# A hybrid decoder layer on one core: the same mixing stage with fewer and narrower products, another order, and a TensorE that starts on zeros

## What is computed

```python
z = rmsnorm(x, mix_norm) @ w_in                      # (256, 1024) @ (1024, IN_WIDTH)
log_f = log_sigmoid(ff + fox_f_bias)                 # 8 columns of z; c = cumsum(log_f)
logit[t,s] = q_t.k_s/8 + c[t] - c[s]                 # q, k: rms-normalised per head
S_t = S_{t-1} diag(w_t) + (S_{t-1} a_t) b_t^T + v_t k_t^T ;  y_t = S_t r_t   # S_0 = 0
y = (y - mean(y)) * rsqrt(var(y) + GN_EPS)           # per head, over its 64 value columns
y = (y * ln_w + ln_b + bonus) * g                    # bonus is from v as it is
x = x + concat([fox_out * sigmoid(fog), y]) @ w_out
logits = rmsnorm(x, moe_norm) @ w_router + b_router  # top 4 of 32 experts per token
x = x + sum of gate * expert(x)                      # clamped SwiGLU, 1024 -> 2 x 1024 -> 1024
x = x + sigmoid(rmsnorm(x) @ w_ple_gate) * (p @ w_ple_proj);  return rmsnorm(x)
```

## Time and profile before

| | |
|---|---|
| median of 3 runs | 1184.32 us (1183.87 to 1185.1) |
| the profiled execution, its own time | 1185.83 us |
| its span | 1184.0 us |
| PE busy | 1136.0 us (96%), 7064 matmuls |
| DVE busy | 283.3 us (24%) |
| ACT busy | 173.2 us (15%) |
| read from HBM | 433.06 MB, 367 GB/s over the span |

### The profile page before, as it was taken

How to read it: one execution, slowest core, us unless ns; L and a number is a source line. 1 busy time by engine, 2 the same in 40 slices (tenths; PEclk the granted TensorE clock), 3 DMA queues, 4 the chain that set the end, 5 groups by cost and what they waited for, 6 DMA issues and landing times.

```text
span 1184.0 us, 16869 instructions
## 1 busy us (share of the span) xinstructions
PE 1136.0 (96%) x7064; PEld 480.0 (41%) x7064; DVE 283.3 (24%) x578; ACT 173.2 (15%) x319; POOL 0.2 (0%) x4
## 2 busy tenths in 40 slices
PE   7999999999999999999999999999999999998997
PEld 6888856433333333333333333333333333332334
DVE  2454734421111111111211211111111111111123
ACT  3322523210100100000010000000000000000015
POOL 0000000000000000000000000000000000000000
PEclk9999999999999999999999999999999999999999
DMA  9751036599999999999999999999999999999970
GB/s 376 324 214 74 22 126 232 218 354 412 427 427 428 427 428 428 429 428 425 430 429 427 429 427 425 429 426 429 428 428 428 429 428 428 429 428 428 427 320 35
DMA packets 34027, 434.76 MB, mean 367 GB/s; under 512 B 4032, under 2 KB 4288, under 8 KB 6976
## 3 DMA queue, kind: packets, MB, share of 16 engines
q1 hardware_dynamic: 33984, 434.13, 87.3%
HBM read 433.06 MB, written 1.05 MB: 367 GB/s over the span
## 4 chain that ended last, share of the span: by engine, by line
PE 48%; DMA 35%; DVE 1%; issue 0%; ACT 0%; SPq 0%; DVEq 0%
DMA ring<-in_we 35%; PE PS L929 33%; PE PS L877 3%; PE PS L892 2%; PE PS L1033 2%; PE PS L753 2%; PE PS L946 1%; PE PS L884 1%; PE PS L980 1%; PE PS L815 0%; PE PS L955 0%; PE PS L548 0%; PE PS L820 0%; PE PS L900 0%; PE PS L776 0%
## 5 line engine op out<-in xcount | busy, mean ns | idle before, releaser
L929 PE MATMUL PS<-ring,FV 128*64 128x512 f32 x2276 | 508.1, 595 | 21.3 <-DMA ring<-in_we 21.3
L929 PEld LDWEIGHTS PS<-ring,FV 128*64 128x64 f32 x2276 | 156.7, 137 | 353.5 <-issue 303.5
L929 PE MATMUL PS<-B,FV 128*64 128x512 f32 x772 | 175.0, 595 | 6.2 <-DMA B<-in_we 6.2
L929 PEld LDWEIGHTS PS<-B,FV 128*64 128x64 f32 x772 | 53.4, 137 | 112.7 <-issue 99.8
L536 PE MATMUL PS<-hT,ring 128*128 128x256 f32 x416 | 93.0, 382 | 0.9 <-ACT hT L1086 0.6
L536 PEld LDWEIGHTS PS<-hT,ring 128*128 128x128 f32 x416 | 78.1, 190 | 12.2 <-ACT hT L1086 0.8
L1573 DVE TENSOR_SCALAR rz<-con,lora 128x64 f32<-128x64 f32 x30 | 7.6, 255 | 305.4 <-PE PS L929 305.4
L1340 DVE TENSOR_TENSOR FV<-PS,prm 128x512 f32<-128x512 f32 x32 | 22.1, 692 | 184.6 <-PE PS L884 184.6
L1655 DVE TENSOR_SCALAR hT<-PS 128x512 f32<-128x512 f32 x32 | 22.1, 692 | 176.8 <-PE PS L929 176.8
L877 PE MATMUL PS<-xq,rz 128*64 128x512 f32 x256 | 62.0, 605 | 0.0
L892 PE MATMUL PS<-B,rz 64*128 64x512 f32 x248 | 61.6, 615 | 0.0
(11 more groups left out here) (273 smaller groups left out, 683.6 us busy)
## 6 DMA issues: line engine op xcount, KB each, us to landing
ring<-in_we SPq DMA_DIRECT2D x135, 2048.0 KB, 23.4
B<-in_we SPq DMA_DIRECT2D x48, 2048.0 KB, 27.6
ring<-in_wz SPq DMA_DIRECT2D x7, 2048.0 KB, 22.7
ring<-in_we SPq DMA_DIRECT2D x14, 1024.0 KB, 7.9
ring<-in_wo SPq DMA_DIRECT2D x2, 2048.0 KB, 7.8
ring<-in_wgate SPq DMA_DIRECT2D x2, 2048.0 KB, 38.8
stash<-in_we SPq DMA_DIRECT2D x1, 2048.0 KB, 13.4
xq<-in_x SPq DMA_DIRECT2D x2, 512.0 KB, 5.3
```

Source lines behind the costliest of these rows:

```text
L929: mm = pe.matmul(PS[64 * h:64 * h + 64, bank_, :], lhs(4 * (q % 2) + k), early[u] if u < units else w[:, k, h, :], start=(first and k == 0 ...
```

## The change

- SP issues both halves of x ahead of `prm`; the first weight piece is issued when the first half of x has landed, the second when the second half has.
- TensorE does 12 products of 128x128 on the zeroed state right after VectorE has zeroed it, and nobody reads them. The wait for all of `hT` goes; the products of `z(0)` wait one by one.
- "bp" leaves its place after z 18 and becomes the second product of "q" 4. Its copy by ScalarE follows "q" 4's.
- The forget-gate columns: weights of eight products side by side (32 columns wide) write four strips of 32 partitions; ScalarE copies the strips, and one product with a 0/1 matrix `fold8` sums the wanted rows ("ff"). z 26 moves ahead of z 22, which is split.
- "t" and "tt": each update only computes the 32 of 64 columns that the level changes, and VectorE adds 512 instead of 1024 columns (strided). "q" k now waits for the second update (`tt`) of the level before, where it waited for the first.
- ScalarE uses one table set (`natural_log_exp_and_others`) for all logarithms and exponentials of the levels, and loads `exp_and_others` once, before the tanh of "fg".
- Chunk 0 leaves out the products with the zero state in "x" and "y".
- The means of y go: "q" 2's second product, which turned v by the identity, turns it by (identity - 1/64) (`centre`, made by VectorE), so that each head's v and with it y comes out centred; the sums, the wait for them and the subtraction are left out.
- Before the routing's last fold there is a product on the first weights of expert 1, which nobody reads; the wait for these weights stands just ahead of it.

The diff, without the tables of step names and without context:

```diff
...
@@ -83,2 +83,2 @@
-MIX_ORDER = [("z", 18), ("bp", 0), ("z", 19), ("ma", 0), ("z", 20), ("aa", 0), ("z", 21), ("z", 22),
-             ("q", 1), ("z", 26), ("qsq", 0), ("ffa", 0), ("ffe", 0), ("t", 1), ("fc", 0), ("qss", 0),
+MIX_ORDER = [("z", 18), ("z", 19), ("ma", 0), ("z", 20), ("aa", 0), ("z", 21), ("z", 26), ("zh", 22),
+             ("q", 1), ("ff", 0), ("qsq", 0), ("z", 22), ("ffa", 0), ("ffe", 0), ("t", 1), ("qss", 0), ("fc", 0),
...
@@ -194,0 +195,6 @@
+        def q_at(k):
+            return 13 if k < 5 else 4
+
+        def level_half(i, k, bit):
+            return b16(i).rearrange("p g (a s b) -> p g a s b", s=2, b=1 << k)[:, :, :, bit, :]
+
@@ -220,0 +227 @@
+        centre = XU[:, 0, 0:CH]
@@ -232,0 +240 @@
+        ff4 = fv2[:, 768:1024]
@@ -235 +243 @@
-            return 2 if n == NZ + 2 else n % 4
+            return 3 if n == NZ else 2 if n == NZ + 2 else n % 4
@@ -334 +341,0 @@
-            sp.dma_start(prm[:, :], t["prm"]).then_inc(s_prm, 16)
@@ -335,0 +343 @@
+            sp.dma_start(prm[:, :], t["prm"]).then_inc(s_prm, 16)
@@ -340,0 +349,2 @@
+                if n < TB:
+                    sp.wait_ge(s_x[n], 16)
@@ -500,0 +511,3 @@
+            pe.wait_ge(s_dve, dve_at["init"])
+            for _ in range(12):
+                pe.matmul(PS[:, 7, 0:P], S[:, 0, 0:P], S[:, 1, 0:P], start=True, stop=True)
@@ -509,2 +521,0 @@
-            pe.wait_ge(s_act, act_at[f"hT{KD - 1}"])
-            pe.wait_ge(s_dve, dve_at[f"hT{KD - 2}"])
@@ -515 +526 @@
-                    pe.wait_ge(s_act, act_at[f"z{n - 4}"])
+                    pe.wait_ge(s_act, act_at[f"z{NZ - 7 if n == NZ else n - 4}"])
@@ -534,0 +546,4 @@
+                    if n == 0 and k % 2:
+                        pe.wait_ge(s_act, act_at[f"hT{k}"])
+                    elif n == 0:
+                        pe.wait_ge(s_dve, dve_at[f"hT{k}"])
@@ -538 +553,3 @@
-                        mm = pe.matmul(PS[0:NHEAD, z_bank(n), 0:SEQ], wff[:, k, :], hT[:, k, :], **flags)
+                        rows = slice(NE * (k % 4), NE * (k % 4) + NE)
+                        four = wff[:, k // 4 * 4:k // 4 * 4 + 4, :].rearrange("p k n -> p (k n)")
+                        mm = pe.matmul(PS[rows, z_bank(n), 0:SEQ], four, hT[:, k, :], start=(k < 4), stop=(k >= 4))
@@ -587,0 +605,3 @@
+            def centred(rows, g):
+                return centre[rows, :]
+
@@ -596,0 +617,3 @@
+            def columns(i, k, bit):
+                return lambda rows, g: level_half(i, k, bit)[rows, g]
+
@@ -606,4 +629 @@
-                if kind == "bp":
-                    pe.wait_ge(s_dve, dve_at["tildes"])
-                    fin(per_head((6, blocks(4), eye, 0)), "bp0")
-                elif kind == "ma":
+                if kind == "ma":
@@ -611 +631 @@
-                    pe.wait_ge(s_act, act_at["bp"])
+                    pe.wait_ge(s_dve, dve_at["tildes"])
@@ -615,0 +636,3 @@
+                elif kind == "ff":
+                    pe.wait_ge(s_act, act_at[f"z{NZ}"])
+                    fin(pe.matmul(PS[0:NHEAD, z_bank(NZ), SEQ:2 * SEQ], c_("fold8"), ff4, start=True, stop=True), "ff0")
@@ -630 +653 @@
-                        pe.wait_ge(s_dve, dve_at[f"t{k - 1}"])
+                        pe.wait_ge(s_dve, dve_at[f"tt{k - 1}"])
@@ -635,2 +658,4 @@
-                        pe.wait_ge(s_act, act_at[f"z{NZ}"])
-                        beside = ((2, blocks(2), eye, 0),)
+                        pe.wait_ge(s_act, act_at["ffh"])
+                        pe.wait_ge(s_act, act_at["z22"])
+                        pe.wait_ge(s_dve, dve_at["cen"])
+                        beside = ((2, blocks(2), centred, 0),)
@@ -639,0 +665,4 @@
+                    elif k == 4:
+                        pe.wait_ge(s_act, act_at["kp"])
+                        pe.wait_ge(s_dve, dve_at["tt3"])
+                        beside = ((4, blocks(4), eye, 0),)
@@ -646,5 +675 @@
-                    if k > 1:
-                        pe.wait_ge(s_dve, dve_at[f"tt{k - 1}"])
-                    else:
-                        pe.wait_ge(s_act, act_at["kp"])
-                    fin(per_head((6, blocks(14), blocks(4), 1), (4, blocks(4), blocks(14), 0)), f"t{k}")
+                    fin(per_head((6, blocks(14), columns(q_at(k), k, 0), 1), (7, blocks(q_at(k)), columns(14, k, 1), 0), n=CH // 2), f"t{k}")
@@ -653,2 +678 @@
-                    pe.wait_ge(s_dve, dve_at[f"tt{k - 1}"])
-                    fin(per_head((4, blocks(4), blocks(14), 0)), f"tt{k}")
+                    fin(per_head((7, blocks(q_at(k)), columns(14, k, 1), 0), n=CH // 2), f"tt{k}")
@@ -720,0 +745 @@
+                        pe.wait_ge(s_act, act_at["bp"])
@@ -723 +748 @@
-                    mm = both(STATE_X, [(ar_(0), of(S, c % 2)), (blk_(2), blk_(3))])
+                    mm = both(STATE_X, [(ar_(0), of(S, c % 2))] * (c > 0) + [(blk_(2), blk_(3))])
@@ -734 +759 @@
-                    mm = both(STATE_Y, [(of(S, c % 2), ar_(1)), (of(XU, 1), blk_(12)), (blk_(3), blk_(13))])
+                    mm = both(STATE_Y, [(of(S, c % 2), ar_(1))] * (c > 0) + [(of(XU, 1), blk_(12)), (blk_(3), blk_(13))])
@@ -759,3 +783,0 @@
-            pe.wait_ge(s_act, act_at[f"y{NC - 1}"])
-            sums(4, b4(8), "mean")
-
@@ -801,2 +822,0 @@
-            pe.wait_ge(s_odd[0], 16)
-
@@ -810,0 +831,2 @@
+            pe.wait_ge(s_odd[0], 16)
+            pe.matmul(PS[:, 5, 0:SEQ], extra[0][:, 0:P], extra[0][:, 0:SEQ], start=True, stop=True)
@@ -1102,2 +1124 @@
-                    fin(act.activation(tmp8[:, 0, :], PS[0:NHEAD, z_bank(n), 0:SEQ], ACT.Identity,
-                                       bias=p_("fb")[0:NHEAD, :]), f"z{n}")
+                    fin(act.activation(ff4, bank(z_bank(n), SEQ), ACT.Copy), f"z{n}")
@@ -1144,0 +1166,4 @@
+                elif kind == "ff":
+                    pe_done("ff0")
+                    fin(act.activation(tmp8[:, 0, :], PS[0:NHEAD, z_bank(NZ), SEQ:2 * SEQ], ACT.Identity,
+                                       bias=p_("fb")[0:NHEAD, :]), "ffh")
@@ -1147 +1172 @@
-                    act.preload_act_table_set("exp_and_others")
+                    act.preload_act_table_set("natural_log_exp_and_others")
@@ -1151,0 +1177 @@
+                    act.preload_act_table_set("exp_and_others")
@@ -1154,3 +1179,0 @@
-                elif kind == "bp":
-                    pe_done("bp0")
-                    fin(act.activation(flat(6), two(6), ACT.Copy), "bp")
@@ -1166 +1188 @@
-                    fin(act.activation(flat(4), two(6), ACT.Copy), f"q{n}")
+                    fin(act.activation(flat(q_at(n)), two(6), ACT.Copy), f"q{n}")
@@ -1170,0 +1193,2 @@
+                    elif n == 4:
+                        fin(act.activation(flat(6), two(4), ACT.Copy), "bp")
@@ -1419,0 +1444,4 @@
+            def update(i, k, bit, b):
+                part = level_half(i, k, bit)
+                return tt(part, bank(b).rearrange("p (g a b) -> p g a b", g=16, b=1 << k), part, ALU.add)
+
@@ -1422 +1450 @@
-                    act_done(f"z{NZ}")
+                    act_done("ffh")
@@ -1454,0 +1483 @@
+                    fin(v.tensor_scalar(centre, c_("eye"), 1.0 / HD, None, ALU.subtract), "cen")
@@ -1466,2 +1495,2 @@
-                        fin(tt(flat(8), two(6), flat(8), ALU.add), f"t{n}")
-                    fin(tt(flat(14), two(4), flat(14), ALU.add), f"tt{n}")
+                        fin(update(8, n, 0, 6), f"t{n}")
+                    fin(update(14, n, 1, 7), f"tt{n}")
@@ -1504 +1532,0 @@
-            pe_done("mean")
@@ -1506,2 +1534 @@
-            fin(v.scalar_tensor_tensor(out=flat(8), in0=two(4), scalar=-1.0 / HD, in1=flat(8),
-                                       op0=ALU.mult, op1=ALU.add), "cent")
+            act_done(f"y{NC - 1}")
@@ -1766,0 +1794 @@
+    put("fold8", p % NE == NHEAD * (p // NE) + np.arange(NHEAD)[None, :])
```

More of the change, by code:

```diff
@@ L72 @@
                        + [("eye", CH), ("causal", P), ("reset", SEQ), ("tri", P), ("ones", SEQ),
-                          ("iota_s", 2 * SLOTS), ("delta", NHEAD), ("iota_i", IW), ("thr", 1), ("fold", NE), ("eval", P),
+                          ("iota_s", 2 * SLOTS), ("delta", NHEAD), ("iota_i", IW), ("thr", 1), ("fold", NE), ("fold8", NHEAD), ("eval", P),
                           ("far", P)])
@@ L96 @@
 PE_STEPS += [f"{kind}{n}" for kind, n in MIX_ORDER if kind not in ASIDE]
-PE_STEPS += ["mean", "var", "xo00", "xo01", "T00", "xo10", "T01", "xo11", "T10", "lt0", "T11", "lg0", "lt1", "lg1", "rank", "pp0", "pp2",
+PE_STEPS += ["var", "xo00", "xo01", "T00", "xo10", "T01", "xo11", "T10", "lt0", "T11", "lg0", "lt1", "lg1", "rank", "pp0", "pp2",
              "rrT", "grT", "count", "pos", "ri", "gi", "ei"]
-ON_VECTOR = {"ma": ["at"], "aa": ["aa", "mq1"], "qsq": ["qsq"], "ffa": ["ffabs"], "fc": ["fc"],
+ON_VECTOR = {"ma": ["at"], "aa": ["aa", "mq1", "cen"], "qsq": ["qsq"], "ffa": ["ffabs"], "fc": ["fc"],
              "qn": ["qn", "ksqf"], "kn": ["kn"]}
-ON_SCALAR = {"bp": ["bp"], "qss": ["qln"], "kss": ["kln"], "qexp": ["qrs"], "kexp": ["krs"],
```

(16 more changed lines are left out.)

## The result

The changed kernel takes **1176.94 us** (median of 4 runs, 1175.76 to 1181.14) beside 1184.71 us for the kernel before: a ratio of 0.9942 (95% interval 0.9924 to 0.996). Two later calls gave 1176.9 (ratio 0.9932, 0.9916 to 0.9949) and 1176.89 us (0.9935, 0.9921 to 0.9949). So 7.8 us are gained beside these runs (7.2 and 7.7 in the later calls) where 11.0 were forecast. The sign and the place were right, and 3.2 us are missing. The time lies outside the forecast's own range of 1171.5 to 1175 us. That it lies inside the wide one, 1168.5 to 1177, is luck: its upper end was set by rivals that did not happen.

A forecast was written before the change was run, and what follows sets the result against it. TensorE's time before 241 us was taken to pass to the end, the expert weights streaming at 428 GB/s after it. Terms of 10.4 us, 11.0 with the clock, gave 1173.3 us, own range 1171.5 to 1175, wide 1168.5 to 1177.

The forecast's parts named there:

- The prediction's own sign against it: An end moving less than the first item's half weight piece, issued at 241.40 us before, would make the whole argument wrong.
- Start, 3.3: Kernel start: x landing sooner and transposes sped up by products on zeros let z 0 begin at 10.6 us, 3.3 less.
- the start gives little: Rival at the start: zeros do not warm TensorE or weights come late, z 0 at 13.1; 1175.8 us, chance 0.13.
- "bp" 2.1: Mixing stage: "bp" no longer between z 18 and z 19, and free in "q" 4: 2.1 us less.
- forget-gate columns 1.9: Mixing stage: 3.55 us become about 1.0, plus 0.45 for the fold and 0.15 for shape changes: 1.9 us less.
- Half columns, 0 on TensorE, VectorE hidden: "t" and "tt" at each level: TensorE gains 0; VectorE's two updates take 1.4 us, hidden behind TensorE's other work.
- both rivals: Level updates: halves save TensorE 4.3 us, 1169, chance 0.12; or updates stay long or late, 3.1 lost, 1176.4, chance 0.16.
- Table set 0.3: Before z 24: three table loads of ScalarE less, which shortens TensorE's wait behind the logarithm by 0.3 us.
- zero state 1.0: Chunk 0: 16 instructions less in each of "x" 0 and "y" 0, together 1.0 us less.
- Means of y, 1.8: TensorE's sums from 194.01 to 195.84 us go: 1.8 us less, with VectorE's chain on y keeping its lead.
- Clock at the routing, 0.6: Routing: if the clock stays up, the first item starts 1.4 us earlier; 0.6 counted for the medians.
- The fall of the clock in the mixing stage: Rival: thinner "t" lowers TensorE's clock in the mixing stage, making the kernel slower, up to 1190 and more; chance 0.04.

The follow-up runs named there:

- e6: Changed kernel with 48 more TensorE instructions on zeros at the start and `wo[1]` issued after z 28 instead of z 21: 1174.46 us.
- e8: Kernel before with only the start of the change (SP's order and waits, products on zeros, single waits of z 0): 1181.53 us.
- e12: Kernel before with the start of the change but without the products on zeros: 1184.0 us.
- e10: Kernel of e6 with the halved columns of "t" and "tt" undone: 1176.34 us.
- e15: Kernel before with `wo[1]` issued after z 28, nothing else changed: 1185.73 us.
- e14: Changed kernel with `wo[1]` issued after z 28 instead of z 21, on the same chip as e13: 1174.34 us.
- e13: Changed kernel unchanged, run on the same chip as e14: 1176.89 us.
- e3: Changed kernel with 8 instead of 12 big products on zeros, all later instructions 16 places earlier: 1180.79 us.
- e5: Changed kernel with 10 large and 14 small products on zeros instead of 12 large, all later instructions 48 places later: 1176.68 us.
- e2: Changed kernel with 11 big and 5 small products on zeros instead of 12 big, all later instructions 16 places later: 1176.43 us.
- e9: Changed kernel with `wo[1]` issued after z 28 instead of z 21, on another chip than e14: 1174.63 us.
- e1: Changed kernel run again as it is, for comparison: 1176.9 us.

## Why the prediction was right or wrong

- **What bounds the kernel**: right. Before 241 us TensorE's time passes to the end, behind it the stream runs at 428 GB/s. In e6 z 27 starts at 139.62 instead of 147.06, 7.4 us earlier, and the median is 9.9 below. The prediction's own sign against it, an end that moves less than the 241.40 mark, seems to be there in the first profile (4.7 against 5.5 us). But from this mark to the end all eighteen profiled executions take 941.5 to 943.9 us, so a difference of 0.8 says nothing; in e6 the mark moves by 10.9 and the span by 12.0.
- **Start, 3.3**: z 0 came 2.9 us earlier in the changed kernel and 3.4 in e8, and e8's time is 2.9 less. In the first profile the step from 0.21 to 0.11 us came only behind the third transpose, in e8 before the first. e12 shows that the zeros are what the transposes' speed hangs on. The rival "the start gives little" is out.
- **"bp" 2.1 and forget-gate columns 1.9**: 2.2, and 2.0 (3.55 against 1.0 and 0.5 for the fold). As work both are right.
- **Half columns, 0 on TensorE, VectorE hidden**: both as forecast, and against both rivals (1.99 for "t", 1.42 for two updates, no wait). What was not seen is that with "bp" in "q" 4 full updates would cost a wait of 1.3 us (e10).
- **Table set 0.3, zero state 1.0**: the wait before z 24 is gone. "x" 0 and "y" 0 are 0.47 us shorter each.
- **Means of y, 1.8**: 1.2. The term was taken as wholly on TensorE's path, and 0.6 of it had covered VectorE's last attention output. The question "what is late next" was asked of VectorE's chain on y, not of the wait for "o" 3 that stood right behind.
- **Clock at the routing, 0.6**: the price was right, the cause is open. From the first product of `w_out` to the mark at 241.40 it is 45.5 to 45.6 us in the three profiled executions where the clock falls (before, e12, e15) and 44.1 to 44.3 in the fifteen others: 1.4 us. The three are those without products on zeros at the start; no run tells how the two hang together. Its share in the medians was not separated.
- **The step that failed is the sum itself.** 10.4 us was work taken out of TensorE's timeline, and its gaps were assumed to stay as they were, 0.3 us in the stage. The measured terms give 2.9 + 2.2 + 2.0 + 0.3 + 0.9 + 1.2 = 9.5; e14, with one transfer moved, is 10.2 below the kernel before, and the 0.7 between them may be the clock at the routing, which is not shown. The change itself has 7.7 (e13), because 2.5 go to instructions that come late. The smaller part of what is missing is in two terms that were sized too high, the start by 0.4 and the means of y by 0.6. Before, the slow forget-gate columns (3.55 us for 16 matmuls) stood among the 256 instructions behind a delayed fetch, which took 5.3 us. Now "q" 1 is the whole of a block, 256 instructions in 2.0 us, its packet stands behind `wo[1]`, and `wo[1]` runs just then. The prediction had read the transfers' share of 0.19 only as a stream that is not full, and had no rival for TensorE waiting for its own instructions.
- Of the rivals none happened. 1176.4 and 1175.8 came near the measured time, by mechanisms that the traces exclude. The fall of the clock in the mixing stage did occur in single executions (106 to 110 us in the one profiled first), but behind a gap, not behind thin work alone: it stands there in three of the nine profiled executions that have a gap (the first, e3 and e5), and in none of the nine without one is there a fall in this stage. That the gap causes it is likely, not shown.

**Still open**: why a fetch is late by some 3 us with no transfer near it in some executions (e2, e9, e14, e5 and the changed kernel, before number 2241), and how the transfer delays the packet. No run here tells. The best version measured is the change with `wo[1]` issued after z 28, 1174.34 and 1174.63 us, 10 us below the kernel before and 2.5 below the change on the same chip.

## What to carry to other kernels

Work taken out of a dense engine takes slack with it. Where 256 small instructions pass in 2 us, look at the instruction queue beside the semaphores, and keep large transfers that nobody waits for out of that stretch. When a wait "issue" stands inside a single product, count all instructions up to it, waits included, in several executions: a fixed spacing points to the fetch. And before a block is written off as pure gain, look at which wait stands right behind it.

## What was not expected of the hardware

- TensorE's instructions come in packets of 16 KB, and gaps of over 0.6 us stood only in front of the executed instructions 1729, 1985, 2241 and 2753, all 193 + 256 k. With no transfer beside it a packet mostly starts 0.5 to 1.2 us after the boundary ahead of it in a stretch of 64x64 products, takes 0.9 to 1.4 us, and behind a gap TensorE goes on 1.2 to 1.5 us after its end. So 256 instructions have about 3 us (an estimate, 0.7 + 1.0 + 1.4); the regular mix here needs 3.8, the densest block 2.0.
- A 2 MB transfer beside it moved the start of such a packet from 1.5 us ahead of the boundary (e14) to 1.1 to 2.0 us behind it (e13, e1).
- A transpose takes 0.21 us per matmul or 0.11, with one step between. With 24 matmuls on zeros ahead the step came at 4.4 us (e8) and 7.8 (the first profile of the change), with 16 and a pause of 1.6 us behind them at 10.1 (e3), with none at 11.2 (e12).
